# Even layer: scores from stacked rows, one attention run with the convolution's products between its steps, and a start by tiles of x

## The reference

```
px, pc = hx @ w_in, hc @ w_in                  # 512 and 256 tokens, 8 chunks of 512 columns
qa, ka, va, ga, bb, cb, ub, gb = split(px, 8)  # the same of pc for the context
qa, ka = axial_rope(qa), axial_rope(ka)        # x only; 8 heads, 2 maps each, 32 deep
s = einsum(q, k) * 32**-0.5                    # x: 768 keys (context + x); context: 256
p = softmax(s);  a = p[:, :, 0] - lam * p[:, :, 1]
out_a = rms_norm(a @ v, subln) * (1 - lam_init) * silu(ga)
out_b = bb * conv3(cb * ub) * silu(gb)         # 3 taps along the tokens
x = x + g_x * rms_norm(concat(out_a, out_b) @ w_out, norm_post)   # and the context likewise
```

## Time and profile before

| | us |
|---|---|
| time, median of 3 runs (lowest, highest) | 1606.98 (1606.38, 1609.61) |
| time of the profiled execution | 1609.18 |
| span of the profiled execution | 1607.4 |
| TensorE busy (matmul) | 1428.3, 89% |
| VectorE busy | 741.8, 46% |
| ScalarE busy | 664.0, 41% |
| GpSimd busy | 433.9, 27% |
| mean granted clock of TensorE | 0.948 of 2.4 GHz |

### The profile page before, as it was taken

How to read it: one execution, slowest core, us unless ns; L and a number is a source line. 1 busy time by engine, 2 the same in 40 slices (tenths; PEclk the granted TensorE clock), 3 DMA queues, 4 the chain that set the end, 5 groups by cost and what they waited for, 6 DMA issues and landing times. The chain is left out here.

```text
span 1607.4 us, 20924 instructions
## 1 busy us (share of the span) xinstructions
PE 1428.3 (89%) x7788; PEld 1146.8 (71%) x7788; DVE 741.8 (46%) x1455; ACT 664.0 (41%) x1434; POOL 433.9 (27%) x340
## 2 busy tenths in 40 slices
PE   5999789999999978599889968999979599999986
PEld 4778567776687666486777756887858478888765
DVE  2154884744314042604299978405130810766423
ACT  4435225644422253521377763321213523665523
POOL 2333244431344313132100001332213134241322
PEclk9999899999999989799999987999989799999998
DMA  4222332100332623231000000121131332211331
GB/s 162 81 77 79 105 133 104 54 27 9 125 130 105 248 90 139 100 130 53 27 1 1 1 1 27 57 74 53 53 118 53 118 128 79 76 50 50 121 141 53
DMA packets 23251, 129.98 MB, mean 81 GB/s; under 512 B 2544, under 2 KB 4208, under 8 KB 10608
## 3 DMA queue, kind: packets, MB, share of 16 engines
q1 hardware_dynamic: 16304, 106.10, 18.5%
q10 hardware_dynamic: 6848, 22.55, 4.0%
HBM read 122.35 MB, written 6.29 MB: 80 GB/s over the span
## 5 line engine op out<-in xcount | busy, mean ns | idle before, releaser
L979 POOL TENSOR_TENSOR w_low<-w_raw,w_high 128x512 fp32r<-128x512 f32 x296 | 386.1, 1313 | 1103.6 <-ACT w_high L1075 1103.5
L1075 ACT CAST w_high<-w_raw 128x512 fp32r<-128x512 f32 x296 | 179.6, 620 | 638.6 <-PE psum L565 469.6
L565 PE MATMUL psum<-x_high,w_high 128*128 128x512 f32 (+1 forms) x696 | 289.0, 415 | 16.8 <-DVE k_low L1711 8.9
L565 PE MATMUL psum<-x_low,w_high 128*128 128x512 f32 (+1 forms) x696 | 275.7, 396 | 0.0
L565 PE MATMUL psum<-x_high,w_low 128*128 128x512 f32 (+1 forms) x696 | 275.0, 395 | 0.0
L565 PEld LDWEIGHTS psum<-x_high,w_high 128*128 128x128 f32 (+1 forms) x696 | 132.3, 190 | 59.6 <-issue 26.1
L565 PEld LDWEIGHTS psum<-x_high,w_low 128*128 128x128 f32 (+1 forms) x696 | 132.2, 190 | 30.7
L565 PE MATMUL psum<-w_high,x_high 128*128 128x512 f32 (+1 forms) x352 | 139.2, 396 | 15.8 <-ACT w_high L1075 8.0
L565 PEld LDWEIGHTS psum<-x_low,w_high 128*128 128x128 f32 (+1 forms) x696 | 132.8, 191 | 21.0 <-issue 0.5
L565 PE MATMUL psum<-w_low,x_high 128*128 128x512 f32 (+1 forms) x352 | 136.6, 388 | 0.0
L565 PE MATMUL psum<-w_high,x_low 128*128 128x512 f32 (+1 forms) x352 | 136.1, 387 | 0.0
(11 more groups left out here) (280 smaller groups left out, 2621.8 us busy)
## 6 DMA issues: line engine op xcount, KB each, us to landing
w_raw<-stream SPq DMA_DIRECT2D x98, 1024.0 KB, 4.8
x_kept<-arena ACTq DMA_DIRECT2D x8, 512.0 KB, 4.3
arena<-x_kept ACTq DMA_DIRECT2D x8, 512.0 KB, 6.3
arena<-bias ACTq DMA_DIRECT2D x8, 448.0 KB, 3.3
arena<-rows ACTq DMA_DIRECT2D x6, 512.0 KB, 5.2
arena<-x SPq DMA_DIRECT2D x4, 512.0 KB, 5.1
arena<-x ACTq DMA_DIRECT2D x4, 512.0 KB, 6.5
arena<-ctx ACTq DMA_DIRECT2D x4, 512.0 KB, 4.8
```

Source lines behind the costliest of these rows:

```text
L565: mm = pe.matmul(o, l, r, start=(first and n == 0 and kind != "fc"), stop=(last and n == len(passes) - 1))
L979: pool.tensor_tensor(WL[:, u % ROOM, :], RAW[:, g % 2, u % 4, :], WH[:, u % ROOM, :].bitcast(F32), ALU.subtract).then_inc(w_lo, 1)
L1075: act.copy(WH[:, u % ROOM, :], RAW[:, g % 2, u % 4, :]).then_inc(w_hi, 1)
```

## The change

1. **Start by tiles.** The columns and the identity come by ScalarE's queue, the other constants behind the first two granules. Each tile of x gets its own root and is turned as soon as it is scaled, into eight open banks. Weight splits stand between the high parts of x; mask copies and the sigmoids of c come after the key weights.
2. **Rotations in between.** Two rotations stand before each of the first four units of `e_v`, in banks 6 and 7. ScalarE and VectorE also split the rotated queries (`E_QH`, and the low part in place).
3. **Stacked rows.** Instead of masked queries, SyncE's queue copies rows inside SBUF: for a head and map three groups of 32 rows, key (high, high, low) and query (high, low, high), 768 wide, each group one request, so 12 requests for a head with its keys and queries. A score is then one product over 96 rows. The places of masked queries, of `b_high` and `b_low` and of the keys of finished heads take them. The requests stand in the queue among the stream's, and wait for steps -1, 1, 10, 13 and 23.
4. **One run of 48 steps**, `EVEN`: for each pair of heads 4 context steps and 8 x steps. Turning lags two steps and the values four, a map has one pair of banks, and ScalarE copies all that is turned.
5. **Convolution products laid in.** `cb`, `ub`, `bb` are cut in 12 chunks of 128 columns (`SLIM`, two units each); of 192 pieces of three products 3, 3, 4 and 6 stand in four steps. The convolution of a tile is made by VectorE in the step after.
6. **After the run**: the last steps stand between units of `gc`, the sums of squares behind its units 4 to 6; root and reciprocal become a logarithm and an exponential on ScalarE. `gc` comes ahead of `e_ga`, and the projection's rows are rolled, so that the convolution's tiles are its inputs 0 to 3.

```diff
-    + [("e_q", 8), ("e_k", 8), ("e_v", 8), ("e_ga", 8), ("cb", 8), ("ub", 8), ("bb", 8), ("gc", 8)]
-    + [("eo0", 8), ("eo1", 8)]
+    + [("e_q", 8), ("e_k", 8), ("e_v", 8)]
+    + [(f"{part}_{j}", 2) for j in range(4) for part in ("cb", "ub", "bb")]
+    + [("gc", 8), ("e_ga", 8), ("eo0", 8), ("eo1", 8)]
...
+    chunks |= halves("eo", np.roll(a["w_out_2"][0], -512, axis=0)) | halves("oo", a["w_out_2"][1]) | {"dft": dft}
...
+        EVEN = [(x, pr, t, hh) for pr in range(HEADS // 2) for x, n in ((False, LT), (True, ST))
+                for t in range(n) for hh in range(2)]
+        PAIR_STEPS = 2 * (LT + ST)
+        keys_of = lambda s: S + L if EVEN[s][0] else L
+        parts_of = lambda s: (0, 4) if EVEN[s][0] else (0,)
+        FEED_E = ((2, 1), (2, 1), (2, 2), (3, 3))
...
+        ROOMS = {
+            "s0": (wide(B_BOTH, 0), wide(B_BOTH, 1)), "s1": (wide(B_BOTH, 2), wide(B_BOTH, 3)),
+            "s2": (wide(QM_FLAT, 0), wide(QM_FLAT, 1)), "s3": (wide(QM_FLAT, 2), wide(QM_FLAT, 3)),
+            "s4": (wide(B_BOTH, 4), wide(QM_FLAT, 4)),
+            **{f"k{pr}": (KH[:, pr, :], KL[:, pr, :]) for pr in range(3)},
+        }
+        STACK_ROOM = {
+            ("k", 0): "s0", ("k", 1): "s1", ("q", 0): "s2", ("q", 1): "s3",
+            ("k", 2): "k0", ("q", 2): "s4", ("k", 3): "s0", ("q", 3): "s2",
+            ("k", 4): "s1", ("q", 4): "s3", ("k", 5): "k1", ("q", 5): "k2",
+            ("k", 6): "k0", ("q", 6): "s4", ("k", 7): "s0", ("q", 7): "s2",
+        }
+        stack = lambda kind, head, m: ROOMS[STACK_ROOM[kind, head]][m]
...
+            def slim(chunk):
+                units = UNITS[chunk]
+                for part, x in enumerate((X, C)):
+                    key = (chunk, part)
+                    acc = open_bank(key, 6 + part)
+                    for k in range(NK):
+                        u = units[k // 4]
+                        pe.wait_ge(w_hi, u + 1)
+                        pe.wait_ge(w_lo, u + 1)
+                        w = slice(P * (k % 4), P * (k % 4) + P)
+                        wh, wl = WH[:, u % ROOM, w], WL[:, u % ROOM, w]
+                        hi, lo = x[k]
+                        o = acc[:, 0:hi.shape[-1]]
+                        for n, (l, r) in enumerate(((wh, hi), (wh, lo), (wl, hi))):
+                            mm = pe.matmul(o, l, r, start=k == 0 and n == 0, stop=k == NK - 1 and n == 2)
+                        if k == NK - 1:
+                            fills_bank(mm, key)
+                            closed.append(key)
+                            if part:
+                                unit_done[u] = (bank_full[fills[key][0]], fills[key][1] + 1)
+                        elif part and k == 3:
+                            used[0] += 1
+                            mm.then_inc(w_used, 1)
+                            unit_done[u] = (w_used, used[0])
+                        yield
...
-            pe.wait_ge(sig("consts_in"), 16 * N_CONSTS)
-            pe.wait_ge(sig("xn"), ST)
-            turns("xT", ST, rows_of(A_X), NK)
+            pe.wait_ge(sig("ident_in"), 16)
+            accs = [next_bank(("xT", k)) for k in range(NK)]
+            for t in range(ST):
+                pe.wait_ge(sig("xn"), t + 1)
+                for k in range(NK):
+                    mm = pe.transpose(accs[k][:, P * t:P * t + P], A_X[:, t, P * k:P * k + P], ident)
+                    if t == ST - 1:
+                        fills_bank(mm, ("xT", k))
...
-            rotate("rope_e", ROPE_E, "perm_e")
-            gemm("e_v", X, C)
...
+            for k in range(NK):
+                if k < 4:
+                    pool[0] = LAST
+                    rotate("rope_e", ROPE_E[2 * k:2 * k + 2], "perm_e", 2 * k)
+                pool[0] = FIRST
+                unit("e_v", k, X, C)
+            pool[0] = ALL
+            def score_even(s):
+                x, pr, t, hh = EVEN[s]
+                w, head, c = keys_of(s), 2 * pr + hh, P * t if x else S + P * t
+                for kind in "kq":
+                    pe.wait_ge(sig(f"{kind}_stacked{hh}"), 96 * (pr + 1))
+                for m in range(2):
+                    key = ("e", "S", s, m)
+                    acc = (open_two if x else open_bank)(key, 2 * m)
+                    q, k = stack("q", head, m)[0:96, c:c + P], stack("k", head, m)[0:96]
+                    for c0 in range(0, w, 512):
+                        c1 = min(c0 + 512, w)
+                        mm = pe.matmul(acc[:, c0:c1], q, k[:, c0:c1], start=True, stop=True)
+                    fills_bank(mm, key)
...
+            pieces, n = (piece for chunk in SLIM for piece in slim(chunk)), len(EVEN)
+            for s in range(n):
+                score_even(s)
+                if s >= 2:
+                    turn_even(s - 2, 0)
+                if s >= 4 and s % 2 == 0:
+                    values_even((s - 4) // 2)
+                feed("e", pieces, FEED_E[s % 4][0])
+                if s >= 2 and EVEN[s - 2][0]:
+                    turn_even(s - 2, 4)
+                feed("e", pieces, FEED_E[s % 4][1])
+            pool[0] = APART_E
+            turn_even(n - 2, 0)
+            values_even(n // 2 - 2)
+            unit("gc", 0, X, C)
+            turn_even(n - 2, 4)
+            unit("gc", 1, X, C)
+            turn_even(n - 1, 0)
+            unit("gc", 2, X, C)
+            turn_even(n - 1, 4)
+            unit("gc", 3, X, C)
+            values_even(n // 2 - 1)
+            for k in range(4, NK):
+                unit("gc", k, X, C)
+                if k < NK - 1:
+                    for i in range(2 * (k - 4), 2 * (k - 4) + 2):
+                        pe.wait_ge(sig("sq"), i + 1)
+                        key = ("ms", SIX[i])
+                        acc = open_bank(key, 4 + i % 2)
+                        fills_bank(pe.matmul(acc[:, :], square("ones_blk"), E_SQ[:, SIX[i], :], start=True, stop=True), key)
+            pool[0] = ALL
+            gemm("e_ga", X, C)
...
+            mixed = [(BH[:, k, :], BL[:, k, :]) for k in range(4)] + X[:4]
+            mixed_c = [(KH[:, k, 0:L], KL[:, k, 0:L]) for k in range(4)] + C[:4]
...
+            def stacked(kind, head):
+                pr, hh = divmod(head, 2)
+                high, low = (KH, KL) if kind == "k" else (E_QH, E_Q)
+                parts = (high, high, low) if kind == "k" else (high, low, high)
+                for m in range(2):
+                    rows = slice(64 * hh + 32 * m, 64 * hh + 32 * m + 32)
+                    for n, part in enumerate(parts):
+                        src = part[rows, pr, :]
+                        sp.dma_start(stack(kind, head, m)[32 * n:32 * n + 32, :].bitcast(F32),
+                                     src if part is E_Q else src.bitcast(F32))\
+                          .then_inc(sig(f"{kind}_stacked{hh}"), 16)
...
+            def stacks(step):
+                if step < 0:
+                    consumed(sp, ("e_k", 4))
+                    sp.wait_ge(sig("ke_lo"), 1)
+                    sp.wait_ge(sig("q_low"), 1)
+                    for kind, head in (("k", 0), ("q", 0), ("k", 1), ("q", 1)):
+                        stacked(kind, head)
+                    return
+                scored(step)
+                if step == 1:
+                    consumed(sp, ("e_k", 5))
+                    sp.wait_ge(sig("ke_lo"), 4)
+                    sp.wait_ge(sig("q_low"), 4)
+                    stacked("k", 2)
+                    stacked("q", 2)
+                if step == PAIR_STEPS - 2:
+                    stacked("k", 3)
+                    stacked("q", 3)
+                if step == PAIR_STEPS + 1:
+                    stacked("k", 4)
+                    stacked("q", 4)
+                    stacked("k", 5)
+                    for hh in range(2):
+                        sp.wait_ge(sig(f"k_stacked{hh}"), 96 * 3)
+                    stacked("q", 5)
+                if step == 2 * PAIR_STEPS - 1:
+                    for hh in range(2):
+                        sp.wait_ge(sig(f"q_stacked{hh}"), 96 * 3)
+                    for head in (6, 7):
+                        stacked("k", head)
+                        stacked("q", head)
+            STACK_STEPS = (-1, 1, PAIR_STEPS - 2, PAIR_STEPS + 1, 2 * PAIR_STEPS - 1)
...
+            rms("x", ST, lambda t: A_X[:, t, :], x_ready, A_JUNK, each=True)
+            for k in range(NK):
+                if k < ROOM:
+                    high(k)
+                ps = filled(act, ("xT", k))
+                act.activation(XH[:, k, :], ps[:, :], ACT.Copy, scale=col("g_pre", k)).then_inc(sig("xT_hi"), 1)
+            ahead("keys")
...
+            for j in range(4):
+                consumed(act, ("e_q", 4 + j // 2))
+                act.wait_ge(sig("rope_e_out"), 2 * j + 1)
+                act.copy(E_QH[:, j, :], E_Q[:, j, :]).then_inc(sig("q_high"), 1)
+                act.wait_ge(sig("rope_e_out"), 2 * j + 2)
+                act.copy(KH[:, j, L:L + S], E_KF[:, j, :]).then_inc(sig("ke_hi"), 1)
```

(23 more changed lines are left out.)

539 lines of the change are left out of this document (236 added, 303 removed).

## The result

The changed kernel takes 1534.4 us (median, 1531.7 to 1536.3) against 1606.7 of the kernel before: ratio 0.9546, 95% interval 0.9525 to 0.9567. The forecast was 1495. So 72 us were gained of the 112 forecast. The profiled execution has a span of 1531.1 us, 76.3 less than before.

A forecast was written before the change was run, and what follows sets the result against it. TensorE was taken to bound the even layer, VectorE to pace 32 attention steps. 41.0 + 196 + 39.6 + 5 + 33.5 = 315.1 us against 419.7 gains 104.6, with the start 113.3: 1495 us, range 1480 to 1516.

The forecast's parts named there:

- the signs that I had named for being wrong: TensorE waiting for a DMA at steps 1 or 13, x steps over 5 us, or a later stage changing length.
- The attention run: Even layer's 48 steps, first score to last fed piece: 183 + 10 + 3 = 196 us, TensorE above 0.92 busy.
- the lump: Convolution on VectorE in steps 7 and 8 of 12: 2.5 us lost four times, 10 us (0 to 13.6).
- the collisions: GpSimd's 24 lows beside VectorE in the attention steps: up to 26 us, a third hit, 3 us on the path.
- The softmax chain: Attention steps: from first score through two maxima and last exponential, 3.7 us, inside the 4.3 of TensorE's step.
- The stacks: First 24 copies on SP's queue, 0.45 us each, 10.8 us of issue: no charge, 0.6 us of room.
- rival (a): The stacking copies come late, first group 9 and second 5 us: +14 us, 1509; chance 0.14.
- The gate stall: Before e_ga, behind gc's gates: the next product needs four banks and loses 5 us (0 to 8).
- The start: Kernel's beginning: first weight product at about 14.6 us, 9.0 us earlier; net gain 8.7 us.
- (b): Rival: VectorE paces the attention steps, 217 us instead of 196, 1516 in all; chance 0.14.
- (c): Rival: nothing lost in lumps, collisions or at the gate, 196 falls to 183 and 5 to 0: 1477; chance 0.09.
- (d): Rival: slower than before, stacking copies run one after another on the queue, about 1780 us; chance 0.03.

The follow-up runs named there:

- norm_short: The spread kernel with the two maps' normalization cut to one scaling of the first map, the second left out; ratio 0.9366.
- spread_low_short: The spread kernel with GpSimd's low parts in the attention run cut to 8 columns; ratio 0.9388.
- low_short: The changed kernel with GpSimd's low parts of the weights split in the attention run cut from 512 columns to 8; ratio 0.9447.
- spread: The changed kernel with the convolution's taps laid one to three at a time behind the normalization of three later steps; ratio 0.9413.
- both_short: The spread kernel with the normalization cut to one scaling and each maximum taken over 128 columns only; ratio 0.9358.
- two_queues: The changed kernel with the first 24 stacking copies split, 12 on SP's queue and 12 issued by ScalarE; ratio 0.9546.
- banks: The changed kernel with e_ga's accumulator banks taken in the order in which gc's gates free them; ratio 0.9509.
- gates_first: The changed kernel with gc's gates ahead of the sub-norm's exponentials and products in ScalarE's and VectorE's queues; ratio 0.9524.
- the early stacks: The changed kernel with the first 24 stacking copies one weight request earlier in SP's queue; ratio 0.9526.

## Why the prediction was wrong

**Right.** The direction, and the pieces that were sums of TensorE's own products in full use: rotations and value products 39.8 for 41.0, gc 41.4 for 39.6, the chain to the projection 16.0 for 16.0. First weight product 14.99 for 14.6. The waits at the convolution and behind the gates were where I said. Of the signs that I had named for being wrong two came true: TensorE waits 3.7 us for a copy at step 1, and x steps 6, 8, 9 and 10 of the twelve last over 5 us (7.3 in step 9, its wait included). It is busy 0.90 of the run where I wanted 0.92.

**The attention run, 196 forecast, 221.7 measured.** Its terms were 183 for TensorE, 10 for the lump, 3 for the collisions. Measured by period and times four:

- TensorE's own work is 47.0 us a period where I had 45.75: 5 us. The 1.2 are changes from one kind of product to the next, 0.15 us ahead of the pieces behind each group of values among them. A small term, mis-sized.
- The softmax chain was to lie inside TensorE's step of 4.3 us. This step of the prediction failed. norm_short shows that it costs 3.1 us a full period, and 9.9 us from the first score to gc's first product (7.5 us by the time, with a wide interval). I had followed the chain from the scores to the last exponential, 3.7 us, and stopped. VectorE does both maxima (1.8) and then the normalization of the step before (0.15, 0.68, 1.02): 3.7 us from the first maximum to its end, and TensorE wants its result right behind the next scores. And 4.3 was a mean: a step with values has 0.70 + 0.75 + 1.46 + 2.1 = 5.0 us of TensorE work, the one after it 3.55, and where the context's steps end two in a row take 3.8 and 3.0. A short step ends before VectorE's chain beside it does, and the transposes at the head of the step behind it wait. Some 1.3 of the 3.1 us are collisions with lows, which stretch the normalization's 0.68 us to 1.29 among others (spread_low_short); the rest stays with the lows cut.
- The lump and the collisions, 10 + 3 forecast, cost 54.8 less 50.1, 4.7 a period, 19 in all: the mechanism was right, the size off. Two things made it larger. I spread the collisions evenly, "a third of them hit"; but the order of work lays the same pair of lows on the context taps every time (1.46 and 1.38 for 0.37 and 0.48: 2.0 us of 4.7, and low_short gave 16 us back). Nor was it a third: with the lows cut VectorE is busy 4.0 us a period less, 16 in the run of the 26 that I had as the most. And I had put no price on the clock: each gap of 3.0 us was followed by some 3 us at 1.2 GHz, 1.5 us lost. low_short's two like periods, 1.5 us apart with the slow stretch and without it, give the same price. What the runs show is that lump, collisions in it and slow clock are the 4.7 us together (spread), and that 2.6 to 4.2 of them go with the collisions alone (low_short); a finer division is argued from the rows.

These make 5 + 10 + 6 = 21 of the 25.7 us. Most of the rest is the late stacks: both_short takes 192.2 us where four periods of 47.0 are 188, and its wait for the last copy is 3.7 us. In the changed kernel the wait is as long, and the granted clock from 784 to 790 us, behind it, is 0.72.

**The stacks.** The step that failed is the issue at 0.45 us. Counted from the first rotation, the copies began after 29.0 us (27.7 forecast), took 15.3 to issue, 0.64 each (10.8), and the last was there after 46.0 (43.3), its landing being shorter (about 2.4 for 4.8). The second score wanted it after 42.3 (43.9): 3.7 us of wait for 0.6 of room. That is rival (a), at a quarter of its price, since only the first group was late. (By its own numbers the rival's first group would have been 10.2 us late, not 9, and VectorE's 6.2 us for a pair of rotations add up to 5.8; neither changes the forecast.) By the Trainium skill (SBUF — State Buffer, "Door 1: The DMA port swizzle") such copies reach 8 of 16 ports, 218 GB/s. From one queue the 24 copies moved 2.36 MB in 15.3 us, 154 GB/s, by their issue. In two_queues the load of weights that they shared the engines with had landed by 775.1 us, and from there to 779.0 the copies alone moved 261 GB/s with the DMA engines' time fully taken (share 1.04):

```profile
775.10:779.00 3.90, 3.90 (x18) 3.21 (x18) 0.02 (x1) 3.65 (x7) 3.29 (x3) 1.00 1.04 261
```

So the trace does not agree with the figure: with several copies at a time, between different groups of 32 rows, the rate is above it. What one copy alone could reach no run shows. A second queue gained nothing all the same: copies issued beside the load took up to 7 us to land, and ScalarE came late. What freed the copies was to start them earlier.

**The gate stall, 5 forecast, 11.5 measured.** I wrote that the next product needs four banks of the gates. The bank rotation gives e_ga's first accumulator the bank whose gate is last, the sixth. I had counted how many banks are free, not which. With the banks in release order the wait is 2.95 us (banks), with two more of 1.5 us in all further on. The exponentials ahead of the gates cost 4.5 us of it (gates_first), as I had it, about 4.

**e_ga and gc.** e_ga took 36.1 us for 33.5: its granted clock is 0.92, since its first 5 us run at 1.2 GHz, behind a stall that the kernel before does not have; 2.6 us, the whole of the difference.

**The start.** The first product came 8.6 us earlier, but the next stage only 4.3 (56.91 for 61.21). From the first product to the last of this stage it took 39.1 us (14.99 to 54.05) in place of 35.2 (23.58 to 58.79), and the wait behind it grew by 0.4. The products now wait for each new part of x, VectorE's lows being 1.1 us apart, and run at 1.2 GHz from 20.5 to 23.8. One of the waits in TensorE's timeline of the changed kernel, and the windows:

```profile
18.18 0.30 PE L591 MATMUL psum<-w_high,x_high 128*128 128x72 f32 x1 [0.57 <-DVE x_low L1865]
```

```profile
15.00:20.00 5.00, 3.96 (x18) 2.56 (x18) 4.12 (x6) 4.59 (x9) 3.33 (x3) 1.00 0.41 118
20.50:23.80 3.30, 3.30 (x10) 2.38 (x8) 0.54 (x2) 0.62 (x1) 1.27 (x1) 0.50 0.62 263
```

In the kernel before, x was complete when the products began, and 23.5 to 51 us are busy without a gap. I let the first product stand for the stage. Half of what was gained at the first product is lost so, by this one pair of profiles; kernels with the same start reach the next stage between 53.9 and 58.8 us.

**The rivals.** (b), VectorE paces the run, had nearly the right run (217) for a reason that doesn't hold: spread changes no work of VectorE's but its place, takes 1.8 us a period off its busy time, and gains 4.7 a period, 21 us in all. By the Trainium skill's rule (SBUF — State Buffer, "Who interferes with whom") a GpSimd operation and a two-input or fast-mode operation of VectorE lock each other out; the taps beside the lows agree, 1.46 for 0.37. The rule taken for each of 24 lows gave the forecast of 1516. Measured, the operations that read PSUM did not stretch (the maxima stay at 0.95), and the collisions cost 16 us because they fell on the lump, 4 where it is spread. (c) and (d) are out.

**What stays open.** Why the early stacks' 4.7 us shrink to 3 at the end, and why the changed kernel is 6.2 us ahead at 738 us when it was 4.3 ahead at 57; both are within the scatter between profiles. Why gc takes 41.4 us for the forecast 39.6 was not looked into. I did not try a second bank for the transposes: none is free.

## What to carry to other kernels

When single-buffered chains cross between engines, price the shortest step, not the mean one, and follow each engine's queue to the operation that the other engine wants next. Lay a lump of side work out one or two operations a step, in the steps where the pacing engine is long anyway: here that was worth 21 us at no cost, some of it because the taps also moved away from another engine's operations. Look at which operations meet that way each time round. When a stage starts behind releases, ask which bank is wanted first and which is freed last, and look for what stands ahead of the release in each queue. A stall costs its length and, where the granted clock falls behind it, half of the slow stretch (here 1.5 us for 3.0 to 3.4).
